# Wide products for the second head group's queries and keys and for the first column block of u

## What is computed

```python
def mixer_attention(x, w_in, b_f, w_out, rel_bias):      # layer 0
    h = x @ w_in                                         # q, k, v of 8 heads (A), q, k, v of 8 heads (B), 8 gates
    o_a = moba_attention(qkv_a[0], qkv_a[1], qkv_a[2], rel_bias)
    o_b = forgetting_attention(qkv_b[0], qkv_b[1], qkv_b[2], log_f)
    return concat(o_a, o_b) @ w_out
...
def mixer_sgu(x, w_in, b_in, ln_g, ln_b, w_s, b_s, w_out):   # layer 1
    h = jax.nn.gelu(x @ w_in + b_in)
    u, v = jnp.split(h, 2, axis=-1)
    v = layer_norm(v, ln_g, ln_b)
    mixed = jnp.einsum('gts,bcsgd->bctgd', causal(w_s), v) + b_s
    return (u * mixed) @ w_out
```

## Time and profile before

| | us |
|---|---|
| median of 3 runs | 998.92 |
| lowest, highest | 998.79, 998.93 |
| the profiled execution, its time | 998.7 |
| its span in the trace | 997.0 |
| TensorE busy | 991.9 (99%) |
| VectorE busy | 703.7 (71%) |
| ScalarE busy | 458.3 (46%) |

### The profile page before, as it was taken

The page is one execution under the profiler, slowest core; times in us unless marked ns, Lnnn a source line. Parts: engine busy times, 40 slices in busy tenths (PEclk is TensorE's granted clock), DMA queues, the critical chain, the costliest instruction groups (busy, mean ns, idle before and its releaser), DMA issues.

```text
span 997.0 us, 13952 instructions
## 1 busy us (share of the span) xinstructions
PE 991.9 (99%) x5370; PEld 850.7 (85%) x5370; DVE 703.7 (71%) x876; ACT 458.3 (46%) x524; POOL 49.7 (5%) x74
## 2 busy tenths in 40 slices
PE   9999999999999999999999999999999999999998
PEld 7888888889878888888888888888898888888887
DVE  5866666878678766666786666668787876666684
ACT  5444344246574544444445443434354553434441
POOL 0700000100001000000010000000210000000010
PEclk9999999999999999999999999999999999999999
DMA  8965656466264675555457755555466676565531
GB/s 289 289 234 168 211 168 212 133 191 185 85 212 164 201 245 192 188 191 194 143 170 270 230 183 201 180 199 182 145 205 218 215 243 213 168 212 171 211 128 43
DMA packets 129799, 191.45 MB, mean 192 GB/s; under 512 B 5448, under 2 KB 95816, under 8 KB 129760
## 3 DMA queue, kind: packets, MB, share of 16 engines
q1 hardware_dynamic: 126432, 180.11, 54.5%
q0 software_dynamic: 3040, 10.54, 3.1%
q10 hardware_dynamic: 288, 0.26, 0.1%
HBM read 189.83 MB, written 1.06 MB: 191 GB/s over the span
## 4 chain that ended last, share of the span: by engine, by line
PE 99%; DMA 0%; DVE 0%; issue 0%; DVEq 0%
PE gu L619 26%; PE gu L627 14%; PE acc L435 10%; PE acc L436 10%; PE acc L437 10%; PE gu L435 6%; PE gu L437 5%; PE gu L436 5%; PE tp L534 2%; PE gu L829 2%; PE gu L919 2%; PE gu L810 2%; PE gu L834 1%; PE gu L924 1%; PE gu L813 1%; PE acc L754 1%
## 5 line engine op out<-in xcount | busy, mean ns | idle before, releaser
L619 PE MATMUL gu<-xT,g_hi 128*128 128x512 f32 x1152 | 274.6, 390 | 0.0
L619 PEld LDWEIGHTS gu<-xT,g_hi 128*128 128x128 f32 x1152 | 215.5, 188 | 44.5 <-ACT g_hi L987 0.2
L1472 DVE TENSOR_REDUCE stage<-gu 128x256 f32<-128x512 f32 x72 | 49.8, 691 | 146.0 <-PE gu L627 146.0
L627 PEld LDWEIGHTS gu<-xT,g_lo 128*128 128x128 f32 x1152 | 147.7, 191 | 5.6
L627 PE MATMUL gu<-xT,g_lo 128*128 128x256 f32 x1152 | 149.4, 283 | 0.0
L1323 DVE TENSOR_TENSOR g_lo<-rawA,g_hi 128x2048 fp32r<-128x2048 f32 (+2 forms) x63 | 136.8, 2173 | 17.4 <-ACT g_hi L987 17.2
L1323 DVE TENSOR_TENSOR g_lo<-rawB,g_hi 128x2048 fp32r<-128x2048 f32 (+1 forms) x64 | 136.5, 2134 | 7.4 <-ACT g_hi L987 7.3
L435 PE MATMUL acc<-d_hi,hT_hi 128*128 128x512 f32 x352 | 138.6, 394 | 0.0
L436 PE MATMUL acc<-d_lo,hT_hi 128*128 128x512 f32 x352 | 137.9, 392 | 0.0
L437 PE MATMUL acc<-d_hi,hT_lo 128*128 128x512 f32 x352 | 137.0, 389 | 0.0
L987 ACT ACTIVATE g_hi<-rawA 128x2048 fp32r<-128x2048 f32 (+2 forms) x64 | 116.0, 1816 | 40.6 <-DMA rawA<-in_ffn_w_up 16.0
(11 more groups left out here) (205 smaller groups left out, 1020.9 us busy)
## 6 DMA issues: line engine op xcount, KB each, us to landing
rawD<-in_ffn_w_down SPq DMA_DIRECT2D x44, 1024.0 KB, 5.5
rawA<-in_ffn_w_gate SPq DMA_DIRECT2D x42, 512.0 KB, 4.0
rawA<-in_ffn_w_up SPq DMA_DIRECT2D x42, 512.0 KB, 5.0
rawB<-in_ffn_w_gate SPq DMA_DIRECT2D x42, 512.0 KB, 4.0
rawB<-in_ffn_w_up SPq DMA_DIRECT2D x42, 512.0 KB, 5.0
rawA<-in_attn_w_in SPq DMA_DIRECT2D x12, 512.0 KB, 4.4
rawB<-in_attn_w_in SPq DMA_DIRECT2D x12, 512.0 KB, 4.5
rawA<-in_ple_w_gate SPq DMA_DIRECT2D x8, 512.0 KB, 4.8
```

What stands on the lines that cost most here:

```text
L619: pe.matmul(bank[:, :], g_hi[:, slot, b, at:at + P], xT[:, b, :, :].rearrange("p i t -> p (i t)"), start=b == 0, stop=False)
L627: done = pe.matmul(bank[:, 0:S], g_lo[:, slot, b, at:at + P], xT[:, b, 0, :], start=False, stop=b == KB - 1)
L1472: dve.tensor_reduce(gates, gu[0][:, :].rearrange("p (i t) -> p t i", i=2), AXX, ALU.add).then_inc(gate_sum, 1)
```

## The change

Attention: chunks 3 and 4 (queries and keys of head group B) go from the narrow to the wide form (WIDE from 2 to 4). VectorE adds their sides, ScalarE no longer copies them out, and the scale of the queries goes into the conversion of chunk 3's weights. VectorE's subtractions for chunks 4 and 5 stand at entries of their own, later than before, and the last one is cut in two halves with a signal each; PE's back part of chunk 5 waits for them one by one. In chunk 2's second half, the sum of gu1 now stands before a subtraction instead of behind it.

Gating layer: u's first chunk goes to the wide form (`u_wide`). VectorE's sums (`u_sum`) write to stage, and ScalarE's `gelu_sum` reads them there. The first two sums stand between the two steps of the norm of v's first half; the conversion of u's second chunk moves ahead of the statistics of v's second half, and the other two sums come behind it.

```diff
 ATTN_COLS = [2, 0, 1, 3, 4, 5]
-WIDE = 2
-WIDE_STEPS = {(1, 0): ("low", 0, 1), (1, 1): (0, 1, "low"), (2, 0): (0, 1, "low"), (2, 1): (0, "low", 1)}
+WIDE = 4
+WIDE_STEPS = {(1, 0): ("low", 0, 1), (1, 1): (0, 1, "low"), (2, 0): (0, 1, "low"), (2, 1): (0, 1, "low"),
+              (3, 0): (0, 1), (3, 1): (0, 1), (4, 0): (0, 1), (4, 1): (0, 1)}
 ATTN_ORDER = [
...
-    ("g", 3, 0), ("pT", 1), ("scores", 0), ("exps", 0), ("inverse", 0),
+    ("g", 3, 0), ("pT", 1), ("scores", 0), ("exps", 0), ("low", 3, 0), ("inverse", 0),
...
-           "sgu": dict(g=6, d=0, u=4, t=2, v=2, a=4, x=4, r=4, ln=2),
+           "sgu": dict(g=6, d=0, u=5, t=2, v=2, a=4, x=4, r=4, ln=2),
...
                         elif e[0] == "g back":
                             c, h = e[1:]
                             if h == 0:
+                                pe.wait_ge(split_b_front, 1)
+                                g_piece((g0 + c) % 2, h, gu[h][:, :], 4, 6)
                                 pe.wait_ge(split_b, g0 + c)
-                            g_piece((g0 + c) % 2, h, gu[h][:, :], 4, KB).then_inc(g_done, 1)
+                                g_piece((g0 + c) % 2, h, gu[h][:, :], 6, KB).then_inc(g_done, 1)
+                            else:
+                                g_piece((g0 + c) % 2, h, gu[h][:, :], 4, KB).then_inc(g_done, 1)
...
+                    def u_wide(c, h):
+
+                        slot = (g0 + c) % 2
+                        for n, (wait, w) in enumerate((((high_a, high_b), g_hi), ((split_a, split_b), g_lo))):
+                            for i_b in range(2):
+                                if n == 0:
+                                    pe.wait_ge(gu_taken[i_b], u0 + c + h)
+                                at = P * (2 * h + i_b)
+                                for b in range(KB):
+                                    if h == 0 and i_b == 0 and b % 4 == 0:
+                                        pe.wait_ge(wait[b // 4], g0 + c)
+                                    if n == 0:
+                                        pe.matmul(gu[i_b][:, :], w[:, slot, b, at:at + P],
+                                                  xT[:, b, :, :].rearrange("p i t -> p (i t)"), start=b == 0, stop=False)
+                                    else:
+                                        done = pe.matmul(gu[i_b][:, 0:S], w[:, slot, b, at:at + P], xT[:, b, 0, :],
+                                                         start=False, stop=b == KB - 1)
+                                if n == 1:
+                                    done.then_inc((wide_full, g_done)[i_b], 1)
+
                     for n, (c, h) in enumerate((c, h) for c in range(4) for h in range(2)):
-                        bank_free(n % 2, u0 + n // 2)
+                        if n < 4:
+                            bank_free(n % 2, u0 + n // 2)
+                        elif n > 5:
+                            bank_free(n % 2, u0 + 4)
...
+                        elif c == 2:
+                            u_wide(c, h)
                         else:
                             u_product(c, h)
...
-                            elif c == 0 and WIDE:
-                                hi_scaled(g0 + 1, h)
+                            elif c in (0, 2):
+                                hi_scaled(g0 + c + 1, h)
...
+                    def gelu_sum(h):
+
+                        for i_b in range(2):
+                            act.wait_ge(gu_taken[i_b], u0 + 3 + h)
+                            done = act.activation(uT[:, 2 * h + i_b, :], stage[:, i_b, S * h:S * h + S],
+                                                  ACT.Gelu_apprx_tanh, bias=bu_col[:, 2 * h + i_b:2 * h + i_b + 1])
+                        done.then_inc(u_ready, 1)
+
...
-                    gelu_u(4)
-                    gelu_u(5)
+                    gelu_sum(0)
+                    gelu_sum(1)
...
+                        elif e[0] == "low":
+                            lo_g(g0 + e[1] + 1, e[2])
+                        elif e[0] in ("low front", "low back"):
+                            rows, signal = ((slice(0, 2), split_b_front), (slice(2, 4), split_b))[e[0] == "low back"]
+                            dve.wait_ge(high_b, g0 + 5)
+                            ks = slice(4 + rows.start, 4 + rows.stop)
+                            low(g_lo[:, (g0 + 5) % 2, ks, :], rawB[:, rows, :], g_hi[:, (g0 + 5) % 2, ks, :])\
+                                .then_inc(signal, 1)
...
+                    def u_sum(h, i_b):
+
+                        dve.wait_ge(*((wide_full, 2 * WIDE + h + 1), (g_done, 2 * g0 + 5 + h))[i_b])
+                        if h == 0:
+                            dve.wait_ge(act_done, a0 + 3 + i_b)
+                        dve.tensor_reduce(stage[:, i_b, S * h:S * h + S],
+                                          gu[i_b][:, :].rearrange("p (i t) -> p t i", i=2), AXX, ALU.add)\
+                            .then_inc(gu_taken[i_b], 1)
+
+                    def u_sums():
+                        u_sum(0, 0)
+                        u_sum(0, 1)
+
...
                     biased(3, 1)
-                    ln_apply_row(v_sgu[:, 0, :], v_sgu[:, 0, :], 0, ln0, vn_ready)
+                    ln_apply_row(v_sgu[:, 0, :], v_sgu[:, 0, :], 0, ln0, vn_ready, between=u_sums)
+                    lo_g(g0 + 3, 0)
+                    lo_g(g0 + 3, 1)
+                    u_sum(1, 0)
+                    u_sum(1, 1)
                     dve.wait_ge(act_done, a0 + 4)
                     ln_stats(v_sgu[:, 1, :], 1)
-                    lo_g(g0 + 3, 0)
-                    lo_g(g0 + 3, 1)
                     ln_apply_row(v_sgu[:, 1, :], v_sgu[:, 1, :], 1, ln0, vn_ready)
```

More of the change, by code:

```diff
@@ L66 @@
     ("g", 2, 0), ("pT", 0), ("g", 2, 1), ("log",),
-    ("g", 3, 0), ("pT", 1), ("scores", 0), ("exps", 0), ("inverse", 0),
-    ("g", 3, 1), ("probs", 0), ("probs", 1), ("scores", 1), ("exps", 1), ("values", 0), ("inverse", 1), ("cum",),
-    ("g", 4, 0), ("probs", 2), ("probs", 3), ("scores", 2), ("exps", 2), ("values", 1),
+    ("g", 3, 0), ("pT", 1), ("scores", 0), ("exps", 0), ("low", 3, 0), ("inverse", 0),
+    ("g", 3, 1), ("probs", 0), ("probs", 1), ("scores", 1), ("exps", 1), ("values", 0), ("low", 3, 1), ("inverse", 1), ("cum",),
+    ("g", 4, 0), ("probs", 2), ("probs", 3), ("scores", 2), ("exps", 2), ("low", 4, 0), ("values", 1),
     ("outputs", 0, 0), ("inverse", 2),
-    ("g", 4, 1), ("probs", 4), ("probs", 5), ("scores", 3), ("exps", 3), ("inverse", 3),
+    ("g", 4, 1), ("probs", 4), ("probs", 5), ("scores", 3), ("exps", 3), ("low front",), ("inverse", 3), ("low back",),
     ("g front", 5, 0), ("values", 2), ("probs", 6), ("probs", 7), ("g back", 5, 0),
@@ L277, in build @@
         wide_full = sem("wide_full")
+        u_ready = sem("u_ready")
+        split_b_front = sem("split_b_front")
         y_ready, y_high, y_low = sem("y_ready"), sem("y_high"), sem("y_low")
@@ L1377, in ln_stats, with ln_apply_row @@
                 ln_moments(h, done)
-            def ln_apply_row(src, dst, h, ln, ready):
+            def ln_apply_row(src, dst, h, ln, ready, between=None):
                 if h == 0:
@@ L1387, in ln_apply_row @@
                 steps[0] += 2
+                if between is not None:
+                    between()
                 dve.wait_ge(rstd_ready, 2 * ln + h + 1)
@@ L1610, in _ @@
                                 for part in WIDE_STEPS[c, h]:
-                                    if part == "low":
+                                    if part == "low" and c == 2:
+                                        lo_scaled_rows(g0 + 3, h, slice(0, 4)).then_inc((split_a, split_b)[h], 1)
+                                    elif part == "low":
                                         lo_g(g0 + c + 1, h)
@@ L1747, in y_gate @@
                         y = t_tok[:, h, 512 * j:512 * j + 512].rearrange("p (b t) -> p b t", b=4)
-                        for bank in range(2):
-                            dve.wait_ge(gu_taken[bank], u0 + 3 + j)
+                        if j == 0:
+                            dve.wait_ge(u_ready, 2)
+                        else:
+                            for bank in range(2):
+                                dve.wait_ge(gu_taken[bank], u0 + 5)
                         dve.tensor_tensor(y, y, uT[:, 4 * j:4 * j + 4, h * P:(h + 1) * P], ALU.mult).then_inc(y_ready, 1)
```

## The result

| | before | changed |
|---|---|---|
| median of 20 runs, us | 998.67 | 1000.40 |
| lowest to highest | 998.27 to 999.35 | 999.18 to 1002.83 |
| profiled execution | 998.7 | 1000.38 |
| its span | 997.0 | 998.7 |

The changed kernel takes 1.0018 times as long (95% interval 1.0013 to 1.0024): 1.7 us slower, with a spread of 3.7 us where there was 1.1. The forecast was 1000.3.

A forecast was written before the change was run, and what follows sets the result against it. The prediction took TensorE (PE), busy 991.9 of 997.0 us, as the bound. Attention's -0.18 us and the gating layer's +1.54 gave +1.36, from a median of 998.92 to 1000.3 us, range 998.9 to 1001.7.

The forecast's parts named there:

- What bounds the kernel, and the saving: PE bounds; six halves in attention and u's first block each save 0.21 us, a ceiling of 1.26 us.
- rival 3: A wide product costs two narrow ones, with the waits on top: 1001.5 us, chance 0.03.
- The wait for gu1: In u's first block, PE waits 1.83 us for the bank that the fourth bias sum frees.
- The small wait at u's second half: PE wants gu0 at 738.21 and gets it at 738.34: 0.13 us.
- No wait at the third block: In u, the narrow block at 745.67 may use gu0 from 745.62: no wait, 0.05 us to spare.
- Attention: Blocks 3 and 4: saving of 0.84 us less waits of 0.21 and 0.45, sum -0.18 us.
- The wait of 0.21 at the third heads' transposes: In attention, PE wants the second head's probabilities at 258.30 and gets them at 258.51: 0.21 us.
- that of 0.45 at the fourth's: In attention after the fourth scores, half a rawB subtraction before the scaling costs 0.3 to 0.65 us, taken as 0.45.
- The two subtractions of the output weights: Gating layer, on VectorE: at about 752 and 754.3, needed from 759, so covered, with no wait.
- Rivals 1 and 5: 1: full saving, no bank or head late, 997.7 us, chance 0.09; 5: rawB early, wait 0.7 us, 999.1, chance 0.08.
- Rival 2: VectorE becomes the bound at u's third block, its lateness coming whole onto PE: 1001.6 us with 1.0 late, chance 0.22.
- Rival 4: Granted clock falls to 1.2 GHz at PE's 1.8 us wait in u's first block: 1004 us, chance 0.03.

The follow-up runs named there:

- The experiment that moves one line: Changed kernel with VectorE's fourth bias sum moved ahead of the statistics of v's first half: 998.78 us, ratio to before 1.0003.
- the longer wait: Changed kernel with the statistics of v's first half computed twice ahead of the fourth bias sum: 1003.05 us, median of 5.
- the output weights early: Changed kernel with VectorE's first subtraction of the output weights moved ahead of the sums and gates of y: 999.57 us, ratio to before 1.0011.

## Why the prediction was right

**The measured time.** 1000.4 against 1000.3 us, in the range. The forecast change was +1.36 us, the measured one +1.73 (the kernel before had 998.67 us in the 20 runs, where the forecast started from 998.92). The direction and the largest term are right by their mechanism. That the totals agree to 0.1 us is luck: attention was too dear by 0.56 us, a wait of 0.82 us was missing, and the starting value was 0.25 us high.

- *What bounds the kernel, and the saving.* Right. PE is busy 1.3 us less for a ceiling of 1.26, which also settles rival 3 (a wide product that costs two narrow ones).
- *The wait for gu1.* Right, and the largest term. Forecast 1.83 us with slow start, the mechanism (bank freed by the fourth bias sum, behind conversion and statistics) as read from the order. The idle time is 1.59; the whole stretch is +1.56 for +1.54 forecast. The experiment that moves one line takes 1.4 to 1.6 us away.
- *The small wait at u's second half.* Forecast 0.13, in the trace 0.1. *No wait at the third block*: right.
- *Attention.* The step that was mis-sized: -0.18 forecast, -0.74 in the trace and -0.71 with this part alone. The wait of 0.21 at the third heads' transposes did not come (258.02 takes 0.66), and that of 0.45 at the fourth's was 0.17 (0.98 against 0.81; 0.32 over the usual 0.66, so the 0.15 in the old entry may well have been this wait already). The walk through VectorE's order was right to about 0.2 us at each point (it put the sums of chunk 4's first half at 251.07, they run from 251.01), but it set VectorE's completion plus 0.36 us against PE with differences of 0.2, finer than it can tell: the third heads' scaling ended at 257.96, where the walk had 258.15, and that was the whole wait.
- *"The two subtractions of the output weights come at about 752 and 754.3; they are needed from 759. Covered."* This step failed. Their times were right (751.44 and 753.65), and they themselves are covered. But a subtraction also frees the raw buffer, and its load comes 3.6 us later than before; I went through this for attention ("nil, up to 0.5") and not for the gating layer. 0.82 us went there in this profile, and between 0.25 and 1.05 us in the six profiles at full clock with the late line and with gamma and beta where they were. No term was given either to the block's two loads being issued 2.20 instead of 3.57 us apart.
- *The rivals.* Rivals 1 and 5 wanted the fourth bias sum to be early; it came 0.65 us earlier than in the kernel before, as PE itself did by 0.70. Rival 2, VectorE as the bound at the third block of u, didn't come; the slower side came from the load instead. Rival 4, the fall of the clock, was put at 0.03 and 1004 us. It doesn't appear in the changed kernel's two profiles, but one of its twenty runs has a mean clock of 0.998 (1001.71 us), and the experiments show it behind waits of 2.0 and 3.0 us, with 1.8 and 2.8 us more; it deserved a larger chance. The probability of slower by over 0.2%, 0.30, was about fair: the ratio is 1.0018. (The chances as listed, with 0.02 for faster, add up to 1.02.)

## What to carry to other kernels

When a product goes to a form that takes two banks, look first at who empties the second one: the bank is wanted half a product earlier than before, and whatever stands before its reader on VectorE becomes a wait of the matrix engine. Of a subtraction or copy that is moved, follow also the buffer that it frees and the load behind that buffer, up to its landing, with the other loads in the air at that time, its own pair's other half among them. Where a gain is a tenth of a per cent, one line's place decides its sign: here the order of VectorE in attention is worth 2.7 us and that of two lines in the gating layer 2.25 us, both more than the 1.26 us that the wide products save.

## What the runs showed of the hardware

- After PE had stood for 2.0 us (one profile) and 3.0 us (one profile), the granted clock was at its lower level: products of 512 columns took 0.43 instead of 0.23 us, over 3.9 us in the one and about 6 us in the other. Behind waits of 1.6 to 1.7 us (seven profiles) and of 0.7 to 0.9 us it was full. A wait of 2 to 3 us thus cost about twice itself, and not in every run (one of five with the longer wait kept a mean of 1.000), which widens the spread. The Trainium skill, "TensorE: Matmul & The Clock Gate", section "A second HAM failure mode: psum-queue depth-cycling", tells of a clock that falls when the engine idles again and again between groups of banks. Of that kind no run here shows a case: both falls in the profiles stand behind one long wait.
- A load of two pieces of 512 KB, its last piece from issue to landing: the first output-weight load of the gating layer, with no other load of SyncE issued in the 7 us ahead of it, took 4.6 to 4.9 us in all profiles. An output-weight load for rawB issued 2.2 to 2.5 us behind rawA's took 5.7 to 7.7 us, in the kernel before too (6.3, the load of 742.83); 3.3 to 4.3 us behind, 5.0 to 5.6. The distance to the load ahead isn't all: the load for rawB at 731 to 735 us stood 3.0 to 5.8 us behind rawA's and took from 4.9 to 6.5 us.
- A load issued 1.35 us behind GpSimd's load of beta (three profiles with the output weights early) took 7.0 to 7.2 us; 3.4 us behind it, 4.8 to 7.3. SyncE's two issues took 0.88 us in most places and between 1.01 and 1.93 us when they stood 3.98 or 3.99 us behind GpSimd's issue for gamma, in seven profiles.
